# Sample's front: state transposes moved behind the scores, the mixer's operands ahead of the softmax, x's roots behind the shares, state stores on GpSimd's queue

## What is computed

```python
z, xBC, dt, q, k, v = split(rmsnorm(h) @ w_in)
# SSD heads (8 heads of 64, state of 128, 2 groups)
xBC = silu(causal_conv4(xBC) + conv_b);  xs, B, C = split(xBC)
dt  = softplus(dt + dt_bias);  cs = cumsum(dt * A)
y   = ((C @ B.T) * exp(cs_q - cs_s)) @ (xs * dt) + (C @ state_ssm) * exp(cs) + D * xs
new_state = exp(cs_last) * state_ssm + B.T @ (xs * dt * exp(cs_last - cs))
y   = group_rmsnorm(y * silu(z))
# sliding-window attention with a sink, over 128 cached + 8 new keys
p   = softmax([q @ k.T * scale + bias, sink]);  a = p @ v
h   = h + concat(y, a) @ w_out
# cross attention, 4 heads of 128, over 256 cached memory tokens
h   = h + softmax(rmsnorm(h) @ w_cq @ mem_k.T) @ mem_v @ w_co
```

## Time and profile before

| | |
|---|---|
| time, median of 3 runs | 2932.24 us (2931.61 to 2936.33) |
| profiled execution, own time | 2932.58 us |
| its span, first to last instruction | 2930.8 us |
| PE busy over the span | 2788.4 us (95%) |
| DVE, ACT, POOL busy | 50%, 40%, 34% |

### The profile page before, as it was taken

One profiled execution on the slowest core, in us unless ns is written; L12 is line 12 of the kernel. 1 busy time (PEld: TensorE's weight loads), 2 busy tenths in 40 slices (PEclk: granted clock), 3 DMA queues, 4 the chain that ended last, 5 costly groups with the idle time before them and its releaser, 6 DMA issues. The chain is left out here.

```text
span 2930.8 us, 34707 instructions
## 1 busy us (share of the span) xinstructions
PE 2788.4 (95%) x13539; PEld 2248.8 (77%) x13539; DVE 1451.0 (50%) x2193; ACT 1168.7 (40%) x1878; POOL 1002.2 (34%) x451
## 2 busy tenths in 40 slices
PE   6789789999999999999999999999999988999998
PEld 3468668878778878878778778888778776888886
DVE  3445565556662275556652475556652445222224
ACT  3344644543352244443452245443542333322222
POOL 1122123333334433333334433333344432333331
PEclk8899989999999999999999999999999998999999
DMA  9554454222223354222223353222223341222221
GB/s 308 192 136 130 145 154 130 77 82 76 70 76 100 94 166 108 80 83 72 72 80 95 111 154 101 79 83 69 80 80 98 116 136 44 79 80 80 83 83 59
DMA packets 415094, 303.05 MB, mean 103 GB/s; under 512 B 48075, under 2 KB 384079, under 8 KB 413890
## 3 DMA queue, kind: packets, MB, share of 16 engines
q1 hardware_dynamic: 412474, 294.41, 33.5%
q10 hardware_dynamic: 1880, 6.34, 0.6%
q0 software_dynamic: 576, 0.07, 0.0%
HBM read 277.90 MB, written 23.85 MB: 103 GB/s over the span
## 5 line engine op out<-in xcount | busy, mean ns | idle before, releaser
L1618 POOL TENSOR_TENSOR w_lo<-w_raw,w_hi 128x1024 fp32r<-128x1024 f32 x398 | 970.0, 2440 | 1767.8 <-ACT w_hi L1632 1767.8
L1632 ACT ACTIVATE w_hi<-w_raw 128x1024 fp32r<-128x1024 f32 x398 | 419.3, 1054 | 552.1 <-PE G L2917 270.6
L2603 PE MATMUL L<-xa_h,w_hi 128*128 128x512 f32 x1184 | 475.5, 402 | 0.0
L2604 PE MATMUL L<-xa_h,w_lo 128*128 128x512 f32 x1184 | 464.9, 393 | 0.0
L2605 PE MATMUL L<-xa_l,w_hi 128*128 128x512 f32 x1184 | 464.4, 392 | 0.0
L2603 PEld LDWEIGHTS L<-xa_h,w_hi 128*128 128x128 f32 x1184 | 224.7, 190 | 54.4 <-issue 6.7
L2605 PEld LDWEIGHTS L<-xa_l,w_hi 128*128 128x128 f32 x1184 | 224.2, 189 | 48.5
L2604 PEld LDWEIGHTS L<-xa_h,w_lo 128*128 128x128 f32 x1184 | 224.4, 190 | 45.8 <-issue 1.0
L2603 PE MATMUL L<-xb_h,w_hi 128*128 128x512 f32 x576 | 231.3, 402 | 14.3 <-DVE xb_l L2039 14.3
L2550 DVE TENSOR_TENSOR sg<-sg,L 128x512 f32<-128x512 f32 x66 | 45.4, 688 | 370.7 <-PE L L2605 370.7
L2604 PE MATMUL L<-xb_h,w_lo 128*128 128x512 f32 x576 | 225.6, 392 | 0.0
(11 more groups left out here) (570 smaller groups left out, 4938.0 us busy)
## 6 DMA issues: line engine op xcount, KB each, us to landing
w_raw<-in_w_down_dram SPq DMA_DIRECT2D x88, 512.0 KB, 3.5
w_raw<-in_w_gate_dram SPq DMA_DIRECT2D x66, 512.0 KB, 3.8
w_raw<-in_w_up_dram SPq DMA_DIRECT2D x66, 512.0 KB, 3.8
w_raw<-in_w_in_dram SPq DMA_DIRECT2D x56, 512.0 KB, 3.8
xt<-xT_dram SPq DMA_DIRECT2D x56, 256.0 KB, 4.1
w_raw<-in_w_gate_dram SPq DMA_DIRECT2D x44, 256.0 KB, 2.8
w_raw<-in_w_up_dram SPq DMA_DIRECT2D x44, 256.0 KB, 3.1
fwin<-in_w_in_dram SPq DMA_DIRECT2D x8, 1156.0 KB, 10.5
```

What stands on the lines that cost most here:

```text
L1618: pool.tensor_tensor(w_lo[:, n % RING, 0:w], w_raw[:, n % RING, 0:w], w_hi[:, n % RING, 0:w].bitcast(F32), ALU.subtract)\
L1632: act.activation(w_hi[:, n % RING, 0:w], w_raw[:, n % RING, 0:w], ACT.Copy)\
L2603: pe.matmul(acc, wh, rh, start=(k == 0), stop=False)
L2604: pe.matmul(acc, wl, rh, start=False, stop=False)
```

## The change

It reorders the front; the arithmetic stays.

1. States behind the scores: PE turns states 0 to 3 right after the scores, 4 and 5 after `xtok`, 6 and 7 after `diff`; ACT copies them in pieces between its other work (three ahead of the conv's Silu, two behind it, one after `ex`, two after `E`).
2. On DVE `dt_u` stands ahead of the convolution, and the mixer's operands with M and `xddS` stand ahead of the softmax's front. y (now from bank 0 of G) stands ahead of the shares' division. PE makes `yoff` and `yd` ahead of the turned shares.
3. In the cross part DVE takes the maximum of the scores at once; x's roots, `diag` and RB come behind the division, `new_state(3)` and `x0_back(0)`. PE spreads the roots after `cpv`, into bank 5, ahead of `x0_chunk(1)`; the turned outputs wait for RB's copy.
4. SP copies the two old caches (480 KB each, from DRAM to DRAM) after it has issued the prompt's first panels, not ahead of `xin0`.
5. The states 2 to 7 are stored by GpSimd's queue, behind its w_lo work, with a semaphore of their own (`state_out`), for which SP and ACT wait in the second phase.

```diff
-                for src, dst in ((cache_swa_k, s_swa_k), (cache_swa_v, s_swa_v)):
-                    sp.dma_start(dst[0, :, 0:WIN - TS]...).then_inc(early["late_out"], 16)
                 sp.wait_ge(f["wq"], 1)
                 for c in range(C):
                     sp.dma_start(xin0[:, c, :], x_prompt[0, c * P:c * P + P, :]).then_inc(f[f"x0_in{c}"], 16)
...
+                for src, dst in ((cache_swa_k, s_swa_k), (cache_swa_v, s_swa_v)):
+                    sp.dma_start(dst[0, :, 0:WIN - TS]...).then_inc(early["late_out"], 16)
+                for n in range(2):
                     bb = PAIRED[n]
                     sp.wait_ge(f["so_sb"], n + 1)
                     sp.dma_start(s_ssm[0, bb]..., stN[:, bb]).then_inc(early["late_out"], 16)
...
-                for n in range(2, NB):
-                    state_out(n)
 
             @blk.gpsimd
...
                     pool.tensor_tensor(w_lo[:, n, :], w_raw[:, n, :], w_hi[:, n, :].bitcast(F32), ALU.subtract)\
                         .then_inc(early["lo_ready"], 1)
+                for n in range(2, NB):
+                    bb = PAIRED[n]
+                    pool.wait_ge(f["so_sb"], n + 1)
+                    pool.dma_start(s_ssm[0, bb]..., stN[:, bb]).then_inc(early["state_out"], 16)
 
             @blk.scalar
...
+                def states_in(a, z):
+                    for bb in range(a, z):
+                        act.wait_ge(f["st_t"], bb + 1)
+                        act.activation(stT[:, bb, :], L[:, bb % 2, :], ACT.Copy).then_inc(f["st_sb"], 1)
+
+                states_in(0, 3)
                 act.wait_ge(f["conv"], 1)
                 act.activation(xbcS[:], convS[:], ACT.Silu).then_inc(f["xbc"], 1)
+                states_in(3, 5)
                 act.wait_ge(f["cum"], 1)
...
+                states_in(5, 6)
                 act.wait_ge(f["diff"], 1)
                 act.activation(ES[:], G[0:S, 2, :], ACT.Exp).then_inc(f["E"], 1)
+                states_in(6, NB)
                 act.wait_ge(f["nmax"], 1)
...
             @blk.vector
...
+                dve.wait_ge(f["dt_e"], 1)
+                dve.tensor_scalar(u, e, 1.0, None, ALU.add).then_inc(f["dt_u"], 1)
                 dve.wait_ge(f["raw"], 1)
                 dve.wait_ge(f["sc_sb"], 1)
...
+                last.then_inc(f["cz"], 1)
+                dve.wait_ge(f["xtok"], 1)
+                dve.tensor_tensor(v3(xdtS[:]), v3(G[0:S, 0, :]), bch(dt_, HP), ALU.mult)
...
+                last.then_inc(f["M"], 1)
+                dve.wait_ge(f["ex"], 1)
+                dve.drain()
+                dve.tensor_tensor(v3(xddS[:]), v3(xdtS[:]), bch(exS[:, HS:2 * HS], HP), ALU.mult)\
+                   .then_inc(f["xdd"], 1)
                 dve.wait_ge(f["sc"], 1)
...
                 new_state(0)
                 new_state(1)
+                dve.wait_ge(f["cs"], 1)
+                dve.tensor_reduce(stx[:, 0, :], G[:, 5, :]..., AX_X, ALU.max, negate=True).then_inc(f["cmax"], 1)
+                new_state(2)
+                dve.wait_ge(f["cexp"], 2)
+                dve.reciprocal(stx[:, 2, :], stx[:, 1, :])
...
+                new_state(3)
+                x0_back(0)
                 dve.wait_ge(f["x0_sq"], C)
                 dve.tensor_scalar(rx[:, 2, 0:C], ssx[:, 0:C], 1.0 / D, EPS, ALU.mult, ALU.add)
                 dve.drain()
...
                     last = dve.tensor_scalar(diag[:, c * P:c * P + P], ident[:], rx[:, 1, c:c + 1], None, ALU.mult)
                 last.then_inc(f["x0_diag"], 1)
...
                 dve.wait_ge(f["cpv"], 2)
                 dve.tensor_copy(oD[:, 1, :], G[:, 4, :]).then_inc(f["od"], 1)
+                dve.wait_ge(f["x0_rb"], 1)
+                dve.tensor_copy(RB, G[:, 5, :]).then_inc(f["x0_rb_sb"], 1)
                 x0_back(1)
...
             @blk.tensor
...
+                states_in(0, 4)
                 pe.wait_ge(f["ze"], 1)
                 pe.wait_ge(f["xbc"], 1)
...
+                states_in(4, 6)
...
                 pe.matmul(G[0:S, 2, :], gtS[:], rdaS[:], start=True, stop=True).then_inc(f["diff"], 1)
+                states_in(6, NB)
...
+                last.then_inc(f["yoff"], 1)
...
+                last.then_inc(f["yd"], 1)
                 pe.wait_ge(f["pn"], 1)
...
-                pe.wait_ge(f["x0_diag"], 1)
-                pe.matmul(G[:, 1, :], ones[:], diag[:], start=True, stop=True).then_inc(f["x0_rb"], 1)
                 state_back(0, 2)
...
                     last.then_inc(f["cpv"], 1)
+                pe.wait_ge(f["cexp"], 2)
+                pe.wait_ge(f["x0_diag"], 1)
+                pe.matmul(G[:, 5, :], ones[:], diag[:], start=True, stop=True).then_inc(f["x0_rb"], 1)
                 x0_chunk(1)
-                pe.wait_ge(f["cexp"], 2)
+                pe.wait_ge(f["x0_rb_sb"], 1)
                 pe.wait_ge(f["od"], 2)
```

More of the change, by code:

```diff
@@ L562, in build @@
         early = {n: whole.enter_context(nc.semaphore("e_" + n))
-                 for n in [f"w_in{r}" for r in range(RING)] + ["hi_ready", "lo_ready", "late_out", "hs_out"]}
-        LATE_OUT = 16 * (2 + 2 + NB)
+                 for n in [f"w_in{r}" for r in range(RING)] + ["hi_ready", "lo_ready", "late_out", "state_out", "hs_out"]}
+        LATE_OUT, STATE_OUT = 16 * (2 + 2 + 2), 16 * (NB - 2)
         PAIRED = [0, 4, 1, 5, 2, 6, 3, 7]
@@ L703, in _ @@
                         .then_inc(early["lo_ready"], 1)
+                for n in range(2, NB):
+                    bb = PAIRED[n]
+                    pool.wait_ge(f["so_sb"], n + 1)
+                    pool.dma_start(s_ssm[0, bb].rearrange("(i h) p n -> (h p) i n", h=2), stN[:, bb])\
+                        .then_inc(early["state_out"], 16)
             @blk.scalar
@@ L979, in _ @@
                 dve.tensor_tensor(yS[:], yS[:], zt[:], ALU.mult).then_inc(f["y"], 1)
+                dve.wait_ge(f["prob"], 1)
+                dve.tensor_tensor(stat[:, 6, :], stat[:, 4, :], stat[:, 5, :], ALU.add)
+                dve.drain()
+                dve.reciprocal(stat[:, 7, :], stat[:, 6, :])
+                dve.drain()
+                dve.tensor_tensor(sS[:], sS[:], stat[:, 7, :].unsqueeze(2).to_broadcast([P, 4, WIN + S]),
+                                  ALU.mult).then_inc(f["pn"], 1)
                 dve.wait_ge(f["ss"], 2)
@@ L1023, in _ @@
                 new_state(1)
+                dve.wait_ge(f["cs"], 1)
+                dve.tensor_reduce(stx[:, 0, :], G[:, 5, :].rearrange("p (g m) -> p g m", g=2), AX_X, ALU.max,
+                                  negate=True).then_inc(f["cmax"], 1)
+                new_state(2)
+                dve.wait_ge(f["cexp"], 2)
+                dve.reciprocal(stx[:, 2, :], stx[:, 1, :])
+                dve.drain()
+                dve.tensor_tensor(sX[:], sX[:], stx[:, 2, :].unsqueeze(2).to_broadcast([P, 2, NMEM]), ALU.mult)\
+                   .then_inc(f["cpn"], 1)
+                new_state(3)
+                x0_back(0)
                 dve.wait_ge(f["x0_sq"], C)
@@ L1118, in _, with states_in @@
                 last.then_inc(f["sc"], 1)
-                pe.wait_ge(f["da"], 1)
-                pe.matmul(G[0:S, 5, 0:HS], leS[:], dtS[:, 8, :], start=True, stop=True)
-                pe.matmul(G[0:S, 5, HS:2 * HS], gtS[:], dtS[:, 8, :], start=True, stop=True)
-                pe.matmul(G[:, 5, 64:64 + NB * HS], ones[0:S, :], dab[:], start=True, stop=True).then_inc(f["cum"], 1)
-                pe.wait_ge(f["rda"], 1)
-                pe.matmul(G[0:S, 2, :], gtS[:], rdaS[:], start=True, stop=True).then_inc(f["diff"], 1)
+                def states_in(a, z):
+                    for bb in range(a, z):
+                        if bb >= 2:
+                            pe.wait_ge(f["st_sb"], bb - 1)
+                        for i in range(4):
+                            last = pe.transpose(L[:, bb % 2, i * P:i * P + P], stN[:, bb, i, :], ident[:])
+                        last.then_inc(f["st_t"], 1)
+                pe.wait_ge(f["st_in"], 16 * NB)
+                pe.wait_ge(f["raw"], 1)
+                states_in(0, 4)
                 pe.wait_ge(f["ze"], 1)
@@ L1151, in _ @@
                 last.then_inc(f["pt"], 1)
-                pe.wait_ge(f["st_sb"], NB)
-                pe.wait_ge(f["cz"], 1)
-                for bb in range(NB):
-                    for g in range(2):
-                        last = pe.matmul(G[S * g:S * g + S, 4, 0:256], Cz[:, bb, g, :],
-                                         stT[:, bb, g * 256:g * 256 + 256], start=(bb == 0), stop=(bb == NB - 1))
-                last.then_inc(f["yoff"], 1)
-                pe.wait_ge(f["M"], 1)
-                for h in range(HS):
-                    last = pe.matmul(G[0:S, 2, h * HP:h * HP + HP], ES[:, h * S:h * S + S],
-                                     xdtS[:, h * HP:h * HP + HP], start=True, stop=True)
-                last.then_inc(f["yd"], 1)
                 pe.wait_ge(f["pt_sb"], 1)
@@ L1266, in _ @@
                 last.then_inc(f["cpt"], 1)
-                pe.wait_ge(f["x0_rb_sb"], 1)
                 x0_chunk(0)
```

101 lines of the change are left out of this document (38 added, 63 removed).

## The result

The changed kernel took 2938.16 us (median of 20 runs, 2933.45 to 2940.24), the kernel before 2932.44 beside it (20 runs, 2929.04 to 2939.02). The ratio is 1.0015, 95% interval 1.0008 to 1.0021: 4.4 us slower, by the ratio (the two medians are 5.7 apart). That is within 0.2%, and 2936.6 on the 2932.24 of before, inside the forecast's own range of 2931 to 2937; the median itself lies 1.2 above it and inside the wider one, to 2938.5. But it is 3 us more than the +1.4 forecast. The profiled execution took 2939.88 us, its span is 2938.1.

A forecast was written before the change was run, and what follows sets the result against it. PE bounds from 151 us on; before that, the front's chain through `mix`, `Bz` and the cross part sets the barrier's end. Chain +2.0, clock +0.4, tail −0.7 and −0.3 give +1.4: 2933.6 us, own range 2931 to 2937, wider 2927.8 to 2938.5.

The forecast's parts named there:

- Convolution at 44.3: First half, DVE: with `dt_u` ahead, the convolution starts at about 44.3 and ends at 51.3, 2.1 us late.
- y at 67.8: First half: y is ready at 67.8 instead of 70.18, 2.3 us sooner.
- Squares 1.2 late, because they stand behind the copies; norm and `mix` keep their distance: First half: ACT's squares of y start at 71.4, not 70.18, behind the shares' copies; `mix` follows at 76.6, not 75.33.
- Hidden rows +0.9: End of first half: `Bz` beside POOL's scalings ends near 85.4, so new hidden rows come 0.9 us later; bounds 0 and 2.0.
- Maximum at once, division done 2.9 us behind its start, w_lo 3.66 behind shares times values: Cross part: maximum at 115.3, division starting at 118.2, shares times values at 119.6 (3.9 us gained), POOL's w_lo at 123.3.
- `diag` stretched by the meeting: Cross part: DVE's `diag`, held beside POOL's w_lo, ends at 128.4 instead of 124.7; chain 2.0 us late, hidden rows' 0.9 included.
- The rival without a meeting (0.22): Cross part: `diag` slips ahead of POOL's w_lo or isn't held; chain 3.8 us better, −2.4, 2929.8 us; chance 0.22.
- Clock after it: +0.4: Cross part: PE idles from 123.3 to 128.4, then half clock costs 0 to 1.5 us; 0.4 taken.
- Loads' order: 0: Loads: old caches no longer ahead of x's rows; an earlier landing is worth nothing, cost 0.
- Tail −1.0: Front's end: POOL's stores at 1.2 us each finish 0.7 sooner than SP, SP's drain saves 0.3; POOL's drain stays 1.54.
- The rivals of a dear or starved issue: Tail, POOL's stores: issue costs by the piece, about +20, 2952 us, chance 0.11; or DVE starves it, +3.8, 2936, chance 0.05.
- the late landing: Behind the barrier: stores land over 4 us late and PE waits, +1 or so, 2934.6 us; chance 0.04.

The follow-up runs named there:

- e10: The kernel before with the changed first half alone (states behind the scores, mixer's operands, y ahead of the division); ratio 0.9996.
- e6: The changed kernel with ACT's squares of y ahead of its two copies of the turned shares; ratio 1.0012 to the kernel before.
- e9: The changed kernel with the softmax's division back ahead of y on DVE alone; ratio 1.0002 to the kernel before.
- e3: The changed kernel with DVE's, ACT's and PE's orders up to `wo` put back as before; ratio 1.0000 to the kernel before.
- e2: The changed kernel with POOL's two w_lo subtractions started only when DVE has written diag; ratio 0.9995 to the kernel before.
- e5: The kernel before with the old caches' copies issued behind the weight panels instead of ahead of x's rows; ratio 0.9980.
- e11: The kernel before with state stores 2 to 7 on POOL's queue and the waits behind the barrier; ratio 0.9997.
- e1: The changed kernel with the six late state stores back on SP, behind the hidden rows; ratio 1.0016 to the kernel before.
- e8: The kernel before with old caches' copies behind the panels and SP's state stores 2 to 4 ahead of the hidden rows' write; 2928.04 us, ratio 0.9980.
- e7: The changed kernel with state stores 2 to 4 on POOL and 5 to 7 on SP; ratio 1.0009 to the kernel before.

## Why the prediction was off by 3 us, step by step

The total stayed in the range, and in part by luck. In the two profiles the exit moved by 7.7 us: hidden rows +5.9, from there to the turned outputs +1.9, to the last state copy +0.6, tail −0.7. The times show 4.4 of it, and why they show less is open.

- *Convolution at 44.3.* Right (44.29).
- *y at 67.8.* 70.2, with the products mostly at half clock; 65.2 with full clock (e10), which is 66.8 with the changed kernel's copy. Mis-sized by the clock.
- *Squares 1.2 late, because they stand behind the copies; norm and `mix` keep their distance.* The first part came out at 0.9 in e10, at 4.1 in the changed kernel. The second failed, and it is the step that failed: `mix` has two suppliers, the norm and PE's shares times values, and only one was followed through. With the division behind y the other was the later one (e6: 4 us off the squares, nothing off `mix`; e9: division back, 5.2 us off `mix`). In the trace of before PE turned the shares 7 us ahead of y's last step, with DVE idle, and its shares times values ended at 71.03, 3.5 us ahead of the norm's end (74.56):

```profile
62.33 0.60 PE L1148 MATMUL G<-ident,sS 128*128 128x128 f32 x4
...
67.02 0.85 DVE L969 TENSOR_TENSOR yS<-G,exS 64x256 f32<-64x256 f32 x2 [6.53 <-PE G L1156]
...
67.97 1.12 PE L1166 MATMUL G<-pnT,kvrow 64*128 64x512 f32 x2
...
69.03 2.00 PE L1169 MATMUL G<-pcT,swV 128*128 128x64 f32 x16
...
73.88 0.68 DVE L985 TENSOR_TENSOR yS<-yS,ssS 64x512 f32<-64x512 f32 x1
```

The order alone would not have made the shares the last, though. From the forecast's 71.4 for the copies, these durations end the shares times values at 74.5, ahead of the norm's 75.8 (estimates). What was missed is that PE waits 3.52 us for the late division and then works at half clock: in e10 the turning takes 1.97 us instead of 1.04, the new keys' part 2.07 instead of 1.12, the cached keys' part 3.67 instead of 2.00. Without these 3.6 us e10's norm would again come last and `mix` 34.9 behind the copy, where before has it (an estimate; in none of the seven profiles with the division behind y did PE keep its clock there). The prediction had such a stretch as its upper bound, 2.6 us on `mix`; it happened in every one of these profiles.

- *Hidden rows +0.9.* In the profile +5.9 from the copy, +3.3 with the products at full clock (e10), mended by e9 to +0.9. `Bz` ended at 88.85, not 85.4, and did not cover the output projection. In time e3 says 4.4 within the changed kernel; alone on the kernel before the timing shows none of it (e10), and this stays open.
- *Maximum at once, division done 2.9 us behind its start, w_lo 3.66 behind shares times values.* Right: at once, 2.7 (119.23 to 121.94), 3.66 (123.45 to 127.11).
- *`diag` stretched by the meeting.* Right in kind and nearly in size: from the last root step to the end of diag 5.1 us, 1.1 without the meeting (e2). The rival without a meeting (0.22) is out.
- *Clock after it: +0.4.* Mis-sized. PE idled 5.45 us; the spreading ran at 2.04 instead of 1.10 us, and from 132 to 136 the clock was 0.50. e2, which takes meeting and clock fall away together, gains 5.6 us from hidden rows to turned outputs.
- *Loads' order: 0.* Right for the changed kernel, where the roots come 6 us later anyway, and the costliest blind spot: the same two lines alone make the kernel before 5.9 us faster (e5). The kernel before paid 3 to 4 us for roots in front of the maximum only because x's rows landed late.
- *Tail −1.0.* −0.7 in the profile (5.40 against 6.09; e11 5.39). The terms differ: store 0.75 us, not 1.2; end of issue 2.1 us sooner than SP's, not 0.7; drain +2.4, named as a possibility and put at 0; and the drain's record starts 0.6 us ahead of the last issue's end, where it started 0.4 behind SP's, 1.0 instead of 0.3. The rivals of a dear or starved issue are out: 0.75 to 0.87 us each, beside DVE's work too. So is the late landing.
- *Sums of the rivals.* With 2.3 us per store the forecast's own terms give +6.1, not +5.8; that changes no chance.

Where the expected gain went: from the scores' start to the turned outputs the moved roots take 19.4 us without the meeting (e2), 2.4 less than the 21.9 of before (1.8 was forecast); the meeting adds 4.0 us on DVE, and 1.7 are left for the clock, 25.1 in all. The first half freed y only in the profiles with the products at full clock, and left `mix` later in all of them, by 0.5 us in e9 and 2.4 to 6.5 in the others; of the 3.1 us won at the tail 2.4 went into POOL's drain.

## What to carry to other kernels

When a step is moved ahead of another, follow every supplier of the next join through its new order, not only the one that was last, and at the clock that it will get: here the norm got all the attention, and the shares, behind a wait of 3.5 us and then at half clock, held `mix`. Before a computation is moved out of the way of a wait, ask why it is late itself; two lines in a DMA queue did for these roots what the reordering on three engines did not. And check what the moved step will run beside: DVE work without PSUM operands can pay the length of a long GpSimd instruction that it lands next to, as `Bz`, `diag` and a step of the roots did.

## What the runs showed of the hardware

- GpSimd's drain at a barrier is 1.54 us without its own stores under way, 3.98 to 4.12 with one issued just before, 1.79 with three, the last issued 5.6 us before: a store issued last by GpSimd lengthened the barrier, and SP's stores did not (1.54 in e1, e8).
- GpSimd issues a store of 512 pieces in 0.75 us (0.87 at most) and a load of 8 pieces in 0.57; of the two loads of 64 pieces the first took 0.75 and the second 0.58. The Trainium skill ("DMA: Bandwidth & Descriptors", "Anatomy of one DMA — SWDGE (gpsimd) path") says that many descriptors can be emitted before the incremental cost shows; by the traces 512 pieces cost 0.18 us more than 8, so it shows and is small.
- A DVE instruction of 0.16 us with both inputs in SBUF took 2.16 beside a GpSimd subtraction of 2.35.
- The same 32 matmuls took 3.67 or 5.12 to 5.45 us with the same code ahead of them. In e1 and e10 the granted clock stayed full after PE's wait of 2.1 us ahead of the scores; in the six others it fell to half within 2 us of the scores' start, although e7 and e9 had kept it full for the 8 us ahead of the copy as well. What decides it is open.
